# Streamed operands 64 bytes behind a multiple of 128, and low weight parts of four projections on VectorE

## The reference

```python
# first block, per layer
u = rms_norm(h, norm_mix_g[layer])
p = u @ w_in[layer]
... # y_a (RWKV-7), y_b (HGRN-2), y_c (sparse attention), each 512 wide, from parts of p
branch = jnp.einsum('bsnc,ncd->bsnd', ys, w_branch[layer])
gates = jax.nn.sigmoid(p_gate.reshape(bsz, seq, N_BRANCH, D_MODEL))
merged = jnp.sum(gates * branch, axis=2)
h = h + merged @ w_o[layer]
u = rms_norm(h, norm_ffn_g[layer])
h = h + conv_glu(u, w_up[layer], conv_w[layer], conv_b[layer], w_down[layer])
# second block, per layer: mix = mLSTM, block attention and latent attention, side by side
x = x + mix @ w_out
h2 = rms_norm_2(x, g_mlp_norm)
x = x + jnp.square(jax.nn.relu(h2 @ w_up)) @ w_down
```

## Time and profile before

| | us |
|---|---|
| median of 3 runs | 2285.23 |
| lowest, highest | 2284.57, 2291.86 |
| span of the profiled execution | 2285.6 |
| TensorE busy | 2026.4 (89%) |
| GpSimd busy | 1405.5 (61%) |
| VectorE busy | 1192.3 (52%) |
| ScalarE busy | 1152.7 (50%) |

### The profile page before, as it was taken

The page is one execution under the profiler, slowest core; times in us unless marked ns, Lnnn a source line. Parts: engine busy times, 40 slices in busy tenths (PEclk is TensorE's granted clock), DMA queues, the critical chain, the costliest instruction groups (busy, mean ns, idle before and its releaser), DMA issues.

```text
span 2285.6 us, 44204 instructions
## 1 busy us (share of the span) xinstructions
PE 2026.4 (89%) x14950; PEld 1910.6 (84%) x14950; DVE 1192.3 (52%) x1649; ACT 1152.7 (50%) x1928; POOL 1405.5 (61%) x1012
## 2 busy tenths in 40 slices
PE   5898898989997999888998997789889989878998
PEld 5888787989997889787998997776789978668998
DVE  2366765247932365775346952277666015765620
ACT  3634235446654654235446653564554446564543
POOL 4672015878986673005887985563389966417996
PEclk8999799999998999799999998897899989789999
DMA  5442003555664542002555664331256644204664
GB/s 166 131 117 67 1 1 94 165 148 159 185 182 126 144 121 77 19 1 65 159 164 144 184 181 140 92 107 56 72 146 184 188 131 134 74 24 139 173 192 144
DMA packets 146627, 274.12 MB, mean 120 GB/s; under 512 B 16273, under 2 KB 16274, under 8 KB 146194
## 3 DMA queue, kind: packets, MB, share of 16 engines
q1 hardware_dynamic: 145584, 267.32, 41.3%
q10 hardware_dynamic: 866, 4.31, 0.5%
HBM read 270.52 MB, written 1.05 MB: 119 GB/s over the span
## 4 chain that ended last, share of the span: by engine, by line
issue 49%; POOL 40%; PE 10%; POOLq 1%; DVE 0%; ACT 0%; ACTq 0%
POOL ring_split L575 40%; PE bank L585 10%; POOLq L572 1%; POOLq L569 0%; ACT arena L1158 0%; POOLq L575 0%; DVE u L1679 0%; DVE arena L1664 0%; ACT rn L1158 0%; DVE u_split L1684 0%; DVE arena L1665 0%; DVE rn L1665 0%; ACTq L245 0%; ACTq L253 0%; POOLq L2279 0%
## 5 line engine op out<-in xcount | busy, mean ns | idle before, releaser
L575 POOL TENSOR_TENSOR ring_split<-ring,hi_ring 128x512 fp32r<-128x512 f32 x1008 | 1405.3, 1413 | 866.9 <-ACT hi_ring L1158 834.4
L1158 ACT ACTIVATE hi_ring<-ring 128x512 fp32r<-128x512 f32 x1008 | 621.9, 630 | 599.3 <-PE bank L585 567.2
L585 PE MATMUL bank<-u_hi,hi_ring 128*128 128x256 f32 (+1 forms) x2480 | 734.4, 296 | 112.2 <-POOL ring_split L575 76.8
L585 PE MATMUL bank<-u_split,hi_ring 128*128 128x256 f32 (+1 forms) x2480 | 715.9, 289 | 0.0
L585 PE MATMUL bank<-u_hi,ring_split 128*128 128x256 f32 (+1 forms) x2480 | 714.9, 288 | 0.0
L585 PEld LDWEIGHTS bank<-u_hi,hi_ring 128*128 128x128 f32 (+1 forms) x2480 | 485.4, 196 | 137.2 <-POOL ring_split L575 95.6
L585 PEld LDWEIGHTS bank<-u_split,hi_ring 128*128 128x128 f32 (+1 forms) x2480 | 487.2, 196 | 1.5
L585 PEld LDWEIGHTS bank<-u_hi,ring_split 128*128 128x128 f32 (+1 forms) x2480 | 486.7, 196 | 1.0
L585 PE MATMUL bank<-arena 128*128 128x128 f32 (+5 forms) x2368 | 343.4, 319 | 31.4 <-ACTq L253 6.6
L585 PEld LDWEIGHTS bank<-arena 128*128 128x128 f32 (+2 forms) x2368 | 308.8, 206 | 70.0 <-issue 31.9
L1158 ACT ACTIVATE arena<-bank 128x512 f32<-128x512 f32 (+4 forms) x262 | 135.9, 519 | 281.5 <-PE bank L585 243.9
(11 more groups left out here) (236 smaller groups left out, 2347.3 us busy)
## 6 DMA issues: line engine op xcount, KB each, us to landing
ring<-in_stream SPq DMA_DIRECT2D x1008, 256.0 KB, 2.8
par<-in_params ACTq DMA_DIRECT2D x5, 637.0 KB, 5.0
h<-in_x SPq DMA_DIRECT2D x1, 1024.0 KB
out<-h ACTq DMA_DIRECT2D x1, 1024.0 KB, 3.9
cst<-in_cst SPq DMA_DIRECT2D x1, 962.0 KB
arena<-in_masks SPq DMA_DIRECT2D x1, 960.0 KB
arena<-in_positions ACTq DMA_DIRECT2D x1, 1.0 KB
```

The lines of the kernel that those rows point to most:

```text
L575: nc.gpsimd.tensor_tensor(ring_lo[:, c, o:o + PIECE * P], x_, hi_ring[:, i % HI_RING, :].bitcast(F32), ALU.subtract).then_inc(pieces_split, 1)
L585: ins = nc.tensor.matmul(o, l, r, start=start, stop=stop)
L1158: return nc.scalar.activation(o, i, f, **kw)
```

## The change

It has two parts.

The first moves what TensorE streams. A spare of 64 bytes (`phase`) after `hi_ring` puts u, u_lo and u_hi 64 bytes behind a multiple of 128, another one puts the arena there, and `Carve` rounds each part up to 128 bytes, so that every tensor of the arena starts 64 behind a multiple of 128. `ring` and `hi_ring` stay.

The second moves work. `SIZES1` and `SIZES2` list the groups of a layer with their blocks, `Owners` says for each piece who makes its low part, and `LoParts.upto` makes those that are VectorE's, written into its program ahead of its wait for the group's bank, with the same lead of three as ScalarE's. VectorE owns the gates from G2 on and the outputs from M1 on, all of WO in the first block and its second half in the second block, U and D. GpSimd keeps the others. TensorE waits on one of two semaphores, by owner. By count VectorE has 62 + 16 + 88 + 44 = 210 of 304 pieces in a layer of the first block, and 8 + 64 + 64 = 136 of 200 in one of the second.

```diff
 MERGE = tuple((f"G{j}{n}", f"M{j}{n}", n, j) for n in BRANCHES for j in range(4))
+BY_VECTOR1 = {m[0] for m in MERGE[2:]} | {m[1] for m in MERGE[1:]} | {f"WO{j}" for j in range(4)} | {f"U{i}" for i in range(22)} | {f"D{j}" for j in range(4)}
+BY_VECTOR2 = {f"WO{j}" for j in range(4)} | {f"U{i}" for i in range(16)} | {f"D{j}" for j in range(4)}
+SIZES1 = [(f"A{i}", 16) for i in range(7)] + [(n, 16) for n in ("Bq0", "Bq1", "Bf0", "Bf1", "Cq0", "Cq1", "Ck")]
+SIZES1 += [("Bi0", 32), ("Cqi", 16), ("Cki", 8), ("Cv", 16), ("Bg0", 16), ("Bg1", 16), (MERGE[0][0], 16)]
+for i in range(len(MERGE)):
+    SIZES1 += [(m[0], 16) for m in MERGE[i + 1:i + 2]] + [(MERGE[i][1], 8)]
+SIZES1 += [(f"WO{j}", 16) for j in range(4)] + [(f"U{i}", 16) for i in range(22)] + [(f"D{j}", 44) for j in range(4)] + [("end", 8)]
+SIZES2 = [("cq0", 16), ("cq1", 8), ("ckv", 16), ("kpe", 8)] + [(n, 16) for n in ("aq", "ak", "av", "qk0", "qk1")]
+SIZES2 += [("uq0", 6), ("uq1", 6), ("uk0", 2), ("uk1", 2), ("uv", 4), ("if", 8), ("mv0", 32), ("mo0", 16), ("mo1", 16)]
+SIZES2 += [(f"WO{j} attention", 8) for j in range(4)] + [(f"WO{j}", 8) for j in range(4)]
+SIZES2 += [(f"U{i}", 16) for i in range(16)] + [(f"D{j}", 64) for j in range(4)] + [("end", 4)]
+assert sum(n for _, n in SIZES1) == BLOCKS1 and sum(n for _, n in SIZES2) == BLOCKS2
...
+class Owners:
+
+
+    def __init__(self, sizes, by_vector, pieces):
+        self.by_vector, at = [False] * pieces, 0
+        for name, n in sizes:
+            for p in range(-(-at // PIECE), -(-(at + n) // PIECE)):
+                self.by_vector[p] = name in by_vector
+            at += n
+        self.total = {v: self.by_vector.count(v) for v in (False, True)}
+
+    def count(self, p):
+
+        return self.by_vector[:p + 1].count(self.by_vector[p])
...
         if p >= self.seen:
-            self.pe.wait_ge(self.split, self.first + (p + 1))
+            made, first = self.made[self.owners.by_vector[p]]
+            self.pe.wait_ge(made, first + self.owners.count(p))
             self.seen = p + 1
...
         h = sb("h", [P, KD, T])
         hi_ring = sb("hi_ring", [P, HI_RING, PIECE * P], F32R)
+        sb("phase", [P, 16])
...
         small = sb("small", [P, 128])
-        ARENA = 36192
-        arena_at = -(-nc.sbuf_base // 32) * 32
+        sb("arena_phase", [P, (64 - nc.sbuf_base) % 128 // 4])
+        ARENA = 36416
+        arena_at = nc.sbuf_base
...
             def __call__(self, n):
-                a = self.at
-                self.at += n
+                a = -(-self.at // 32) * 32
+                self.at = a + n
...
         def _(pool):
-            n = (layers[0] * CH1 + layers[1] * CH2) // RING
-            per_round = RING * CHUNK // PIECE
-            with pool.Fori(0, n) as r:
-                for i in range(per_round):
-
-                    pool.wait_ge(hi_written, r * per_round + (i + 1))
-                    c, o = i * PIECE // CHUNK, i * PIECE % CHUNK * P
-                    x_ = ring[:, c, o:o + PIECE * P]
-                    nc.gpsimd.tensor_tensor(ring_lo[:, c, o:o + PIECE * P], x_, hi_ring[:, i % HI_RING, :].bitcast(F32), ALU.subtract).then_inc(pieces_split, 1)
+            for n, own, before in ((layers[0], own1, 0), (layers[1], own2, layers[0] * PIECES1)):
+                if not n:
+                    continue
+                with pool.Fori(0, n) as l:
+                    for q, by_vector in enumerate(own.by_vector):
+                        if by_vector:
+                            continue
+                        pool.wait_ge(hi_written, l * len(own.by_vector) + (before + q + 1))
+                        c = q % RING
+                        nc.gpsimd.tensor_tensor(ring_lo[:, c, :], ring[:, c, :], hi_ring[:, q % HI_RING, :].bitcast(F32), ALU.subtract).then_inc(lo_by_pool, 1)
 
...
 
+            class LoParts:
+
+
+                def __init__(self, ends, own, first):
+                    self.ends, self.own, self.first, self.at = ends, own, first, 0
+
+                def upto(self, name, lead=LEAD):
+
+                    stop = min(self.ends[name] + lead, max(self.ends.values()))
+                    for q in range(self.at, stop):
+                        if not self.own.by_vector[q]:
+                            continue
+                        dve.wait_ge(hi_written, self.first + (q + 1))
+                        c = q % RING
+                        V.tensor_tensor(ring_lo[:, c, :], ring[:, c, :], hi_ring[:, q % HI_RING, :].bitcast(F32), ALU.subtract).then_inc(lo_by_vector, 1)
+                    self.at = max(self.at, stop)
+
...
+                    lo.upto(output)
                     bank = B.wait(dve, output)
                     dve.wait_ge(S["gate_ready"], i + 1)
...
                 for j in range(4):
+                    lo.upto(f"WO{j}")
                     bank = B.wait(dve, f"WO{j}")
                     o = h[:, 2 * j:2 * j + 2, :].rearrange("p a t -> p (a t)")
...
                 for i in range(23):
                     if i < 22:
+                        lo.upto(f"U{i}")
...
                 for j in range(4):
+                    lo.upto(f"D{j}")
                     bank = B.wait(dve, f"D{j}")
                     o = h[:, 2 * j:2 * j + 2, :].rearrange("p a t -> p (a t)")
```

More of the change, by code:

```diff
@@ L253, in release, with __init__ @@
         eng.sem_inc(self.free[self.slot[name][0]], 1)
+class Owners:
[8 more added lines that the diff above has]
+        return self.by_vector[:p + 1].count(self.by_vector[p])
 class Weights:
-    def __init__(self, pe, lo_ring, hi_ring, split, used, first, ends):
-        self.pe, self.lo_ring, self.hi_ring, self.split, self.used, self.first = pe, lo_ring, hi_ring, split, used, first
+    def __init__(self, pe, lo_ring, hi_ring, owners, made, used, ends):
+        self.pe, self.lo_ring, self.hi_ring, self.owners, self.made, self.used = pe, lo_ring, hi_ring, owners, made, used
         self.ends, self.seen, self.next, self.pending, self.told = ends, 0, 0, 0, 0
+        self.sizes = {}
     def take(self, name, n):
@@ L268, in take @@
         self.ends[name] = -(-self.next // PIECE)
+        self.sizes[name] = self.sizes.get(name, 0) + n
         return q
@@ L368, in build @@
         inputs_in, params_in, stored = sem("inputs_in"), sem("params_in"), sem("stored")
-        hi_written, pieces_split, pieces_used = sem("hi_written"), sem("pieces_split"), sem("pieces_used")
+        hi_written, pieces_used = sem("hi_written"), sem("pieces_used")
+        lo_by_pool, lo_by_vector = sem("lo_by_pool"), sem("lo_by_vector")
         arrived, gathered, released, ready = sem("arrived"), sem("gathered"), sem("released"), sem("masks_ready")
@@ L393, in build @@
         small = sb("small", [P, 128])
-        ARENA = 36192
-        arena_at = -(-nc.sbuf_base // 32) * 32
+        sb("arena_phase", [P, (64 - nc.sbuf_base) % 128 // 4])
+        ARENA = 36416
+        arena_at = nc.sbuf_base
+        assert arena_at % 128 == 64
         arena = sb("arena", [P, ARENA])
@@ L534, in build @@
         ends1, ends2 = {}, {}
+        own1, own2 = Owners(SIZES1, BY_VECTOR1, PIECES1), Owners(SIZES2, BY_VECTOR2, PIECES2)
         u_parts = (u_hi, u_lo)
@@ L676, in _ @@
             with pe.Fori(0, layers[0]) as l:
-                W = Weights(pe, ring_lo, hi_ring, pieces_split, pieces_used, l * PIECES1, ends1)
+                W = Weights(pe, ring_lo, hi_ring, own1, {False: (lo_by_pool, l * own1.total[False]), True: (lo_by_vector, l * own1.total[True])}, pieces_used, ends1)
                 B = b1
@@ L955, in _ @@
                 W.skip(BLOCKS1)
+                assert list(W.sizes.items()) == SIZES1
                 layer_end(pe, l + 1, False)
@@ L969, in _ @@
             with pe.Fori(0, layers[1]) as l:
-                W = Weights(pe, ring_lo, hi_ring, pieces_split, pieces_used, l * PIECES2 + layers[0] * PIECES1, ends2)
+                W = Weights(pe, ring_lo, hi_ring, own2, {False: (lo_by_pool, l * own2.total[False] + layers[0] * own1.total[False]),
+                                                         True: (lo_by_vector, l * own2.total[True] + layers[0] * own1.total[True])}, pieces_used, ends2)
                 B = b2
@@ L1151, in _ @@
                 W.skip(BLOCKS2)
+                assert list(W.sizes.items()) == SIZES2
                 layer_end(pe, l + (layers[0] + 2), False)
@@ L1701, in _ @@
                 C, B = Chain(dve, S["dve_chain"]), b1
+                lo = LoParts(ends1, own1, l * PIECES1)
                 dve.wait_ge(params_in, (l + 1) * 16)
@@ L2080, in _ @@
                 C, B = Chain(dve, S["dve_chain"]), b2
+                lo = LoParts(ends2, own2, l * PIECES2 + layers[0] * PIECES1)
                 dve.wait_ge(params_in, (l + (layers[0] + 1)) * 16)
```

## The result

The changed kernel takes 2306.0 us (median of 4 runs, 2302.1 to 2313.4), the kernel before 2286.8 us in the same comparison: 1.0081 times as long, with a 95% interval of 1.0057 to 1.0104. It is slower, by 19 us, where 10 us of gain were forecast. The time lies in the stated range (2250 to 2318), near what the first rival gave (2310).

What follows compares the result with a forecast made beforehand. TensorE was taken to bound the first block's up projection, GpSimd the second's. The terms -25.4 - 21.8 + 50 + 1.4 - 8.8 - 5.1 gave -9.7 us, so 2275.5 us, with a range of 2250 to 2318.

Steps and rivals of the forecast that it cites:

- the first rival: Wherever TensorE bounds: placement gives little, 118 ns or still 120 a matmul; 2310 or 2322 us; chance 0.27.
- Up projection of the first block: VectorE's fourth low part queues behind convolution and `hidden[i-1]`: 7.0 us a step instead of 5.76, 50 us lost.
- Streaming rate: Where TensorE bounds, streams placed 64 behind a multiple of 128 take 113.3 ns a matmul; 25.4 us gained.
- the second block's up projection: TensorE becomes the bound instead of GpSimd: 5.44 us instead of 6.12 for 48 matmuls, 21.8 us gained.
- the down projections: Both blocks: matmuls gain 5.4 ns (first) or 3.7 ns (second) from the new rate; 11.6 us gained.
- First block, from u to the merges: Some 550 u matmuls a layer gain 6.7 ns each: 3.7 us a layer, 7.4 us in both.
- Merges, start: TensorE stands some 14 us before G2 for VectorE, then 7 us at 1.2 GHz; 1.4 us lost for two layers.
- Output projection of the first block: Wait for the last split of `merged` falls from 3.72 to some 2.4 us and 2.4 GHz holds; 8.8 us gained.
- Second block, ahead of the up projection: About 400 matmuls a layer gain 6.7 ns, and `mix` 0.5 us: 3.2 us a layer, 6.4 us in both.
- The wait for `mix_lo`: Second block: TensorE's wait of 1.26 us goes; counted among small items of 5.1 us gained for both pairs.
- the rule named beside it: Trainium skill's 262 cycles, 109 ns, for 256 columns with no address term: by it the streams would not change.

Runs made afterwards that it cites:

- e3: The changed kernel with the low parts of U0 to U21 of the first block made by GpSimd again; 2255.3 us, 0.9849 of before.
- e4: The changed kernel with VectorE making the fourth piece of U(i+1) right behind the convolution of U(i), in the first block; 2271.2 us, 0.9924 of before.
- e2: The changed kernel with the start addresses of the kernel before, so VectorE's low parts alone; 2330.1 us, 1.0183 of before.
- e5: As e1, but both rings of weights also start 64 bytes behind a multiple of 128, like the streams; 2297.5 us, one run.
- e6: As e1, but u and all arena tensors start at multiples of 128 bytes, like the weights; 2286.3 us, one run.
- e1: The changed kernel with every low part made by GpSimd again, so the new start addresses alone; 2269.1 us, 0.9912 of before.
- e9: As e3, but GpSimd also makes the low parts of the merges, G0 to M11; 2253.5 us, 0.9842 of before.
- e10: As e3, but VectorE makes the low parts of G2, M1 and G3 earlier, between steps of its merge preparation; 2242.3 us, 0.9802 of before.
- e12: As e1, but streams start at multiples of 128 bytes and both rings of weights 64 behind one; 2269.6 us, one run.
- e7: As e1, but u and all arena tensors start 32 bytes behind a multiple of 128; 2268.4 us, one run.

## Why the prediction was wrong

**Up projection of the first block: right.** 20 steps of 7.0 us were forecast from the order of VectorE's program, 7.05 came, and e3 and e4 show the cause. Its 50 us outweigh all the rest, and this was sized to 1 us in both layers.

**Streaming rate: the step that failed.** "I take 113.3, because `merged` has the same weight tiles as almost all streams". The row was real, but `merged` is streamed in the earlier trace rows behind a wait after which the rate came out at 113.3 and then held. I read a state of the stretch as a property of the address. The other row in hand, `latents` with 118.3 ns, was 0.5 ns from the truth, and I had set it aside because of its narrower weights. The signs were in the trace of before: `merged` itself runs at 118 ns in its first pieces, ahead of its wait, and I had a single tensor for the fast end. What the runs showed in its place is 117.5 ns in the mean for u and 117.7 for `hidden` in the changed kernel; `hidden` had 117.9 before, so it gained next to nothing. The cost: 4.5 ns on all that TensorE bounds. It made the second block's up projection 5.65 us a step instead of 5.44 (0.21 x 32 = 7 of the 9.7 us missing there), the down projections 7.8 us poorer and the merges 3.3 us a layer longer (62 x 12 x 4.5 ns).

**First block, from u to the merges: the rate again, and the clock.** Forecast -7.4 us, measured +3.3. Both kernels wait here at many places and the granted clock falls after them. Windows over this stretch of the first and the second layer of e4, whose program there is that of the changed kernel:

```profile
28.00:369.00 341.00, 306.01 (x2239) 285.05 (x2240) 197.57 (x345) 158.24 (x268) 126.20 (x91) 0.91 0.25 69
727.00:1072.00 345.00, 309.21 (x2238) 287.20 (x2238) 195.71 (x345) 158.08 (x269) 126.30 (x91) 0.90 0.25 68
```

The same instructions take 341 and 345 us at mean clocks of 0.91 and 0.90. The granted clock is 0.50 for 61.4 us of the one and for 68.5 of the other, and half of that difference is 3.6 of the 4.0 us. Taking half the time at 0.50 off the time of both layers leaves 624.3 to 624.8 us at distance 0 (before, e2, e5, e6), 622.5 in the changed kernel and 619.9 to 623.4 in the others at distance 64 (e1, e3, e4, e9, e10, e12). So the placement gave 2 us of work here where 7.4 were forecast, about what 550 matmuls times 2.2 ns, twice, make; and the clock, 0.50 for 133 us instead of 122, took 5. The traces (after, e1, e3, e4, e9, e10) give 340.9 to 345.3 us a layer here, before 340.9 and 344.7. Such a stretch can't be sized to 4 us from one execution, and a term of 3.7 us a layer was too fine for it.

**Merges, start: right in kind.** A wait of 14 us was forecast, 13.3 measured from start to start (13.06 idle):

```profile
387.25 1.23 DVE L1698 TENSOR_TENSOR ya_lo<-arena,ya_hi 128x1024 fp32r<-128x1024 f32 x1
388.61 1.90 DVE L1747 TENSOR_TENSOR ring_split<-ring,hi_ring 128x512 fp32r<-128x512 f32 x3
389.36 0.58 PE L622 MATMUL bank<-u_hi,hi_ring 128*128 128x256 f32 x1 [13.06 <-DVE ring_split L1747]
```

The granted clock was 0.50 for the next 3.6 us, not for 7. That is 1.6 us a layer better, the rate 3.3 worse, and VectorE's preparation ended a microsecond earlier than forecast.

**Output projection of the first block: the wait right, the clock wrong.** The wait is 2.27 us, as forecast (2.4):

```profile
481.07 0.39 PE L622 MATMUL bank<-merged_hi,hi_ring 128*128 128x256 f32 x1 [0.81 <-DVE ring_split L1747]
484.31 0.39 PE L622 MATMUL bank<-merged_hi,hi_ring 128*128 128x256 f32 x1 [2.27 <-DVE merged_lo L1698]
```

But 485:488 shows 0.52: "after a wait of some 2.4 us I expect 2.4 GHz to hold" failed, and no row of before had stood behind it. The clock is at 0.50 for 3.4 us here, for 6.8 before. In e10 the same wait of 2.27 us left the clock at 1.00. The length of the last wait alone does not decide it. The first row is a wait that I had missed: a low part behind the splits in VectorE's queue. Together 5.6 us of the forecast 8.8 went.

**Second block, ahead of the up projection: right in the sum, by luck** (-9.8 against -8.9). At 117.8 ns the 400 matmuls a layer give 1.8 us of the 6.4 forecast; another 5 us came with the placement, which no term had and no run explains (e1). The wait for `mix_lo`, 1.26 us in the first of the two layers of before, was credited to both. It is gone, but six matmuls ahead of its place TensorE now waits in both layers for VectorE's low part:

```profile
1686.02 0.38 PE L622 MATMUL bank<-mix_hi,hi_ring 128*128 128x256 f32 x1 [1.13 <-DVE ring_split L1747]
```

In its up projection the place of the fourth piece in VectorE's queue was judged right: TensorE never waits there (1720:1790), which gave 13 of the 23 us.

**The chances.** The rival that came was given 0.27, with 2310 us at 118 ns; 2306 came. It came by another way than the rule named beside it, though: placement does act, by 2 to 3 ns in e6 against e7 and e1. The Trainium skill, "TensorE: Matmul & The Clock Gate", section "Back-to-back issue gap", gives 262 cycles for 256 columns with no term for the address, but as the gap of an isolated matmul; for a stream with loads of weights, as here, it says that both set the spacing. No long stretch of these matmuls came under 113.3 ns, 272 cycles. The other section of the Trainium skill that the prediction names, "Operand start alignment" in "SBUF — State Buffer", says of its own measurements that they timed nothing, so it could not speak against an effect. The measurements decide.

## What to carry to other kernels

Before moving work from an idle engine to a faster one, write down what stands ahead of it in the new queue and when its user wants it: here an instruction half as long cost 1.4 us a step because it stood behind the convolution, the product and the split, and one placed ahead of two of them (the product and the split of `hidden`) cost 0.3 us a step. Leave such pieces with the engine that has nothing else to do wherever the time is bound elsewhere, and give the faster engine only what the slow one can't keep up with. Before taking a rate from one tensor, look whether it holds on both sides of a wait. And before crediting a difference of a few us to a change, compare for how long the granted clock was low in the two traces.

## What the runs showed of the hardware

- **Matmul spacing depends on the distance between moving operand and weights within 128 bytes.** For the streams u and `hidden`, 128x256 float32 against 128x128 weights: 119.8 to 120.0 ns at distance 0 and on average at 96, 117 at 32, 117.8 at 64. Moving either side does it (e5, e12). `mix` and `latents` do not follow it: 117.9 and 118.1 ns at distance 0 (e6), 117.7 and 118.2 at 64 (e1). What makes the difference is not known.
- **At distance 64 there is a second rate, 113.3 ns.** 14 of 102 long stretches of the changed kernel have it, 5 of 62 in e1, 9 of 101 in e4. It mostly changes at a wait and holds to the next, but not always: in e1 u goes from 117.8 to 113.3 ns at 1879.9 us behind a single distance of 132 ns, with no idle time recorded, and in e4 at 578.2 us with no longer distance at all. Against weights of four columns u has 113.3 to 113.7 ns at every distance, in 26 of 28 groups of 48 matmuls. What settles it stays open; no run here tried to steer it. If all ran at it, e10 would gain some 40 us at most, an estimate: its 6,900 starts of u at 117.7 ns and 2,600 of `hidden` at 117.1.
- **Scatter of one program.** The stretch from u to the merges takes 341 us in one layer and 345 in the next (e4, above), and e10's runs range from 2237.7 to 2249.3 us, those of the changed kernel from 2302.1 to 2313.4, while e1's stay within 2268.6 to 2270.3. Within e4 the clock makes 3.6 of the 4.0 us. For the scatter between executions the clock and the rate drawn at a wait would do it; that was not tested by itself.
- **The granted clock after a wait** is not set by the length of that wait alone. After one of 2.27 us it was 0.52 in the changed kernel and 1.00 in e10, at the same matmul of the same projection; after one of 2.70 us 0.50 in e5 and 1.00 in e6.
- **VectorE and GpSimd**: with GpSimd silent for most of the time, the low part took VectorE 690 ns in the mean of 692, and a cast of 128x256 0.29 us. In e3, where GpSimd works beside it, the same cast takes 1273 ns and the subtraction 1402 (0.43 us alone), as the grouped instructions of 540:640 have them (count, busy us, mean ns, idle before):

```profile
L1698 DVE TENSOR_TENSOR hidden_lo<-arena,hidden_hi 128x256 fp32r<-128x256 f32 x18 | 25.2, 1402 | 0.6
L1697 DVE CAST hidden_hi<-arena 128x256 fp32r<-128x256 f32 x18 | 22.9, 1273 | 0.6
```

  Only the subtraction has two inputs in SBUF, which is what the rule of the Trainium skill cited in the prediction speaks of; the cast has one and is slowed by as much. It costs e3 nothing: TensorE is the bound there, and VectorE's slower work fits beside it.
